# A gated retention and conv mixer: rotation by swapped copies, centred values, and another order of small steps

## The reference

```python
p = h @ w_in
rq, rk, rv, rg, gq, gf, gi, gg, ca, cb, gates = jnp.split(p, bounds, axis=-1)
q = _rope(heads(rq, 4), positions)            # t1*cos - t2*sin, t1*sin + t2*cos
k = _rope(heads(rk, 4), positions) * (128 ** -0.5)
o = _retention(q, k, heads(rv, 4))            # sum_{s<=t} gamma_h^(t-s) (q_t.k_s) v_s
mu = o.mean(-1, keepdims=True)
o = (o - mu) * lax.rsqrt(jnp.square(o - mu).mean(-1, keepdims=True) + LN_EPS)
u_a = o * ret_norm_g * jax.nn.silu(rg)

o = _hgrn2(silu(gq), logf, -expm1(logf), gi)  # S_t = diag(f_t) S_{t-1} + k_t v_t^T, o_t = S_t^T q_t
o = o * lax.rsqrt(jnp.square(o).mean(-1, keepdims=True) + LN_EPS)
u_b = o * hgrn_norm_g * jax.nn.silu(gg)

u = _causal_dwconv(ca * jax.nn.sigmoid(cb), conv_w, conv_b)   # 31 taps
u_c = jax.nn.silu(_layer_norm(u, conv_ln_g, conv_ln_b))
y = sum over three branches of sigmoid(gates[:, :, i]) * (u_i @ w_branch[i])
return y @ w_out
```

## Time and profile before

| | us |
|---|---|
| median of 3 runs | 3512.76 (3499.04 to 3517.75) |
| the profiled execution | 3506.1 |
| its span, first to last instruction | 3504.3 |

### The profile page before, as it was taken

One profiled execution on the slowest core, in us unless ns is written; L12 is line 12 of the kernel. 1 busy time (PEld: TensorE's weight loads), 2 busy tenths in 40 slices (PEclk: granted clock), 3 DMA queues, 4 the chain that ended last, 5 costly groups with the idle time before them and its releaser, 6 DMA issues. The chain is left out here.

```text
span 3504.3 us, 38804 instructions
## 1 busy us (share of the span) xinstructions
PE 3335.8 (95%) x15280; PEld 2662.9 (76%) x15280; DVE 2126.9 (61%) x2701; ACT 1306.1 (37%) x1684; POOL 616.4 (18%) x496
## 2 busy tenths in 40 slices
PE   8899999999999999989999998999898999989997
PEld 6577788886677788877777876888676777768886
DVE  8853566448654766477556746554676557465545
ACT  4664322234663322233332234243433322343323
POOL 2222222121212212201000132010201001320002
PEclk9999999999999999999999999999999999999999
DMA  4122555322123454232112222222221112222221
GB/s 133 37 68 85 186 192 192 108 96 65 39 78 132 181 192 168 91 112 72 61 55 66 91 99 89 96 96 93 75 85 60 61 55 90 96 73 96 97 97 71
DMA packets 72180, 344.43 MB, mean 98 GB/s; under 512 B 25152, under 2 KB 26048, under 8 KB 35648
## 3 DMA queue, kind: packets, MB, share of 16 engines
q1 hardware_dynamic: 70416, 339.12, 28.2%
q0 software_dynamic: 576, 2.33, 0.2%
q10 hardware_dynamic: 1008, 0.51, 0.1%
HBM read 340.51 MB, written 2.10 MB: 98 GB/s over the span
## 5 line engine op out<-in xcount | busy, mean ns | idle before, releaser
L893 PE MATMUL bank<-Hhi_b,whi_b 128*128 128x512 f32 x2976 | 1220.2, 410 | 62.3 <-ACT Hhi_b L2048 22.1
L894 PE MATMUL bank<-Hhi_b,wlo_b 128*128 128x512 f32 x2976 | 1170.5, 393 | 0.0
L900 PE MATMUL bank<-Hlo_b,whi_b 128*128 128x512 f32 x2976 | 1160.9, 394 | 0.8 <-DVE Hlo_b L2329 0.8
L871 DVE TENSOR_TENSOR wlo_b<-raw_b,whi_b 128x2048 fp32r<-128x2048 f32 (+2 forms) x290 | 626.6, 2161 | 487.7 <-ACT whi_b L865 487.5
L893 PEld LDWEIGHTS bank<-Hhi_b,whi_b 128*128 128x128 f32 x2976 | 566.3, 190 | 212.8 <-issue 43.7
L894 PEld LDWEIGHTS bank<-Hhi_b,wlo_b 128*128 128x128 f32 x2976 | 566.6, 190 | 125.4 <-issue 13.8
L900 PEld LDWEIGHTS bank<-Hlo_b,whi_b 128*128 128x128 f32 x2976 | 563.9, 190 | 124.9 <-DVE Hlo_b L2329 4.2
L865 ACT ACTIVATE whi_b<-raw_b 128x2048 fp32r<-128x2048 f32 (+2 forms) x290 | 511.6, 1764 | 368.4 <-PE bank L900 364.4
L893 PE MATMUL bank<-Uhi_b,whi_b 128*128 128x512 f32 x1024 | 405.7, 396 | 11.3 <-POOL Ulo_b L982 11.3
L894 PE MATMUL bank<-Uhi_b,wlo_b 128*128 128x512 f32 x1024 | 399.8, 390 | 0.0
L900 PE MATMUL bank<-Ulo_b,whi_b 128*128 128x512 f32 x1024 | 386.2, 390 | 0.0
(11 more groups left out here) (257 smaller groups left out, 3460.3 us busy)
## 6 DMA issues: line engine op xcount, KB each, us to landing
raw_b<-in_w SPq DMA_DIRECT2D x234, 1024.0 KB, 4.9
ada_b<-in_wada SPq DMA_DIRECT2D x48, 1024.0 KB, 7.0
raw_b<-in_w SPq DMA_DIRECT2D x40, 512.0 KB, 3.8
raw_b<-in_w SPq DMA_DIRECT2D x16, 768.0 KB, 4.3
rel_b<-in_rel SPq DMA_DIRECT2D x128, 24.0 KB, 2.4
X_keep<-in_x SPq DMA_DIRECT2D x4, 512.0 KB, 9.5
decay_b<-in_decay POOLq DMA_DIRECT2D x2, 1024.0 KB, 6.9
out<-X_keep SPq DMA_DIRECT2D x8, 256.0 KB, 2.0
```

The source lines that it names most:

```text
L871: self.nc.vector.tensor_tensor(self.wlo[n % RAW_SLOTS][:, 0:words], self.raw[n % RAW_SLOTS][:, 0:words], self.whi[n % HI_SLOTS][:, 0:words ...
L893: self.nc.tensor.matmul(out, whi[:, k, cols], xhi, start=(k == 0), stop=False)
L894: self.nc.tensor.matmul(out, wlo[:, k, cols], xhi, start=False, stop=False)
L900: mm = self.nc.tensor.matmul(out, whi[:, k, cols], xlo, start=False, stop=(k == nk - 1))
```

## The change

- The rotation matmul goes. On evacuation of an rq or rk chunk, ACT copies the upper half of the partitions, negated, to the lower half of a new buffer `qr`, and the lower half to the upper, and then the whole to `qf`. The "rrot" item is issued right there: POOL multiplies `qf` by cos in place, DVE multiplies `qr` by sin in place and adds the two.
- The "omean" group goes. The four transposes of a retention head's values become plain matmuls of the same tiles with the matrix (identity - 1/128), so that the head's output has mean zero over its channels. The square is taken by ACT from the bank ahead of the copy.
- The head's end has three parts: "oss" without the reciprocal, "orec" (the reciprocal) and "oend". When another head follows, "orec" joins its second group and "oend" its fourth; behind the last gated head they are groups of their own with an empty one between. `finish` no longer takes these two.
- Taps: one beside each group of a retention head, where it was two (one at "oss"); one beside the levels 1, 3, 5 and 7, where it was none; "orec" ahead of its group takes the free number.
- The gate and projection panels of branch 0 all come ahead of those of branch 1.

The diff, cut to its core:

```diff
-    return heads, mixed(0, 0) + mixed(1, 0) + mixed(0, 1) + mixed(1, 1), mixed(2, 0) + mixed(2, 1)
+    return heads, mixed(0, 0) + mixed(0, 1) + mixed(1, 0) + mixed(1, 1), mixed(2, 0) + mixed(2, 1)
 def taps_beside(group, free):
-    if not kinds or kinds == ["oend"]:
+    if not kinds or kinds[0] == "orec":
         return free
...
-    if group[0][2] == "r":
-        return 1 if "oss" in kinds else 2
-    return 0
+    if kinds[0] == "level":
+        return group[0][4] % 2
+    return 1 if group[0][2] == "r" else 0
...
         def finish(branch, h):
-            while any(item[2:4] == (branch, h) for group in chain for item in group):
+            while any(item[2:4] == (branch, h) and item[0] not in ("orec", "oend") for group in chain for item in group):
                 step()
         def follow(*groups):
-            if chain and chain[-1][0][0] == "oend":
-                groups = (groups[0] + chain.pop(),) + groups[1:]
+            if chain and chain[-1][0][0] == "orec":
+                orec, oend = chain.pop()
+                groups = groups[:1] + (groups[1] + (orec,), groups[2], groups[3] + (oend,)) + groups[4:]
             chain.extend(groups)
...
             s.add("evp", l, t, i)
+            if t in ("rq", "rk"):
+                run(("rrot", l, "r", i, t))
...
-                    first = [(item("rrot", "rq"),), (item("rrot", "rk"),), (item("vt2"),)]
-                    first += [(item("rscore", j),) for j in range(TT)] + [(item("rpv"),), (item("omean"),)]
+                    first = [(item("vt2"),)]
+                    first += [(item("rscore", j),) for j in range(TT)] + [(item("rpv"),)]
...
-                follow(*first, (item("oss"),), (item("oend"),))
+                follow(*first, (item("oss"),), (item("orec"), item("oend")))
+                if (b, i) == ("h", 3):
+                    orec, oend = chain.pop()
+                    chain.extend(((orec,), (), (oend,)))
... (POOL, "rrot")
-                ng.tensor_tensor(buf(("t1", l, b, h, t)), buf(("qf", l, t, h)), cos[:], ALU.mult)\
+                ng.tensor_tensor(q, q, cos[:], ALU.mult).then_inc(*mark("pool", ("q cos", l, t, h)))
... (ACT, "evp")
+                elif t in ("rq", "rk"):
+                    half = P // 2
+                    reuse(act, qr_)
+                    act_e.activation(buf(qr_)[0:half], z[half:P], ACT.Copy, scale=-1.0)\
+                        .then_inc(*mark("act", ("qr low", l, t, i)))
+                    act_e.activation(buf(qr_)[half:P], z[0:half], ACT.Copy).then_inc(*mark("act", qr_))
+                    reuse(act, qf_)
+                    act_e.activation(buf(qf_), z, ACT.Copy).then_inc(*mark("act", qf_, ("free", job)))
... (DVE, "rrot")
-                nv.tensor_tensor(t2[:], k.out_of(rot)[:], sin[:], ALU.mult)\
-                nv.tensor_tensor(buf(name), u, t2[:], ALU.add)\
+                dve.wait_ge(*after("qr", l, t, h))
+                nv.tensor_tensor(v, v, sin[:], ALU.mult).then_inc(*mark("dve", ("q sin", l, t, h)))
+                dve.wait_ge(*after("q cos", l, t, h))
+                dve.wait_ge(*after("q sin", l, t, h))
+                nv.tensor_tensor(buf(name), u, v, ALU.add)\
... (DVE: "omean" goes; "oss" keeps the scaling of ON)
-                k.root(None, dve, ("oss", l, b, h), rs, 1.0 / P, EPS2)
+            elif kind == "orec":
+                l, b, h = a
+                k.root(None, dve, ("oss", l, b, h), ("rs", l, b, h), 1.0 / P, EPS2)
... (PE: "rrot" and "omean" go)
-                nt.matmul(k.out_of(job)[:], rot128[:], buf(("qf", l, t, h)), start=True, stop=True)\
-                nt.matmul(k.out_of(job)[:], keep.ones[:], ON[:], start=True, stop=True).then_inc(*mark("pe", job))
                 for t in range(TT):
-                    mm = nt.transpose(k.out_of(job)[:, tile(t)], buf(v)[:, tile(t)], keep.ident[:])
+                    if b == "r":
+                        mm = nt.matmul(k.out_of(job)[:, tile(t)], buf(v)[:, tile(t)], center[:], start=True, stop=True)
+                    else:
+                        mm = nt.transpose(k.out_of(job)[:, tile(t)], buf(v)[:, tile(t)], keep.ident[:])
... (host)
+    center = (np.eye(P) - 1.0 / P).astype(np.float32)
```

More of the change, by code:

```diff
@@ L622, in evacuate @@
                 s.temp("qf", 4, ("qf", l, t, i))
+                s.temp("qr", 2, ("qr", l, t, i))
             if t in ("rv", "gi"):
@@ L1732, in block_two @@
     um = mem.again(ulo_at + 4 * SEQ * 4, ulo_at + 8 * SEQ * 4)
-    t1 = [um.put(f"t1{i}", [P, SEQ]) for i in range(2)]
-    t2 = um.put("t2", [P, SEQ])
+    qr = [um.put(f"qr{i}", [P, SEQ]) for i in range(2)]
+    um.at += SEQ * 4
     pos_i = um.put("pos_i", [P, SEQ], I32)
```

71 lines of the change are left out of this document (19 added, 52 removed).

## The result

The median fell from 3512.53 us (3499.04 to 3517.75, four runs) to **3449.44 us** (3448.62 to 3450.02, four runs); the ratio is 0.9831, with a 95% interval of 0.9808 to 0.9853. The forecast was 3443, inside 3420 to 3466. The profiled execution took 3449.65 us against 3506.1, so 56.5 us less; the medians differ by 63.1. The 6.6 us between them come from the kernel before, whose runs scatter by 18.7 us and whose profiled execution lies 6.4 us (0.18%) under its median, while the new kernel's lies on it.

A forecast was written before the change was run, and what follows sets the result against it. PE, busy 95%, was taken as the bound. Matmuls (18.2 us) plus waits and tails (27.1 in layer 0, 24.5 in layer 1) made 69.8 off 3506.1; 3436.3 times 1.0019 (profile to median) gave 3443 us, range 3420 to 3466.

The forecast's parts named there:

- ACT: Rotation evacuation: three copies instead of one, +1.1 us 16 times, costed at nothing on PE; 18 us without cover.
- The rotation's waits: First scores' waits for the rotated key: 5.8 us go in layer 0 and 7.0 in layer 1.
- The forced steps of "finish": PE's waits for the square, 1.91 us at a retention head and 1.3 behind the first gated head: 3.2 us a layer go.
- The reciprocal: Moved behind level 1 of the next gated head: waits fall from 8.9 to 4.1 us a layer, 4.8 gone.
- Rival A: The reciprocal only moves; waits return at levels 2 and 3, so the levels gain nothing: 3462 us, chance 0.17.
- First branch together: First panel reading the gated heads' split comes four panels later; its 3.50 us wait for POOL goes in both layers.
- The start of layer 0: Mixer's first panels: panel 3 starts 2.7 us later, yet 1.8 us of excess goes besides the matmuls; bounds -2.7 and +4.
- New waits: DVE late at heads 0 and 2: 1.5 us in layer 0, 3.5 in layer 1; range 0 to 10.
- rival D: DVE stands at each of 16 rotations for ACT and POOL, delaying queued work 4.0 us plus tail: 3531 us, chance 0.02.
- The tails: Slow products after PE's long waits, 16 and 15 us in the two layers: 9.5 us of each go.
- Rival C: Each of 16 sine multiplies on DVE waits 1.6 us more for POOL's cosine, PE with it: 3469 us, chance 0.06.
- B: Only the matmuls' 18.2 us count; every wait removed comes back elsewhere: 3495 us, chance 0.06.

The follow-up runs named there:

- the added matmuls: Changed kernel with each head's sum of squares computed twice, 8 more fp32 matmuls a layer: 3460.65 us, 0.9862 of the kernel before.
- The five undone parts: Changed kernel with one part put back each: gate order 3461.86 us, tap numbers 3469.70, two-part head's end 3468.05, rotation in the chain 3461.44, mean step 3457.89.

## Why the prediction was right or wrong, point by point

**The number.** 3449.44 against 3443 is nearer than the working deserves. In the profiled executions 56.5 us came of 69.8, a miss of 13.3, and in the mixers 52.8, a miss of 17.0. The first block's 3.7 us made up for some of it. The factor 1.0019 made up for 6.9: it added 6.7 us for a profiled execution under its median, and the new kernel's lies 0.2 above. So nearly two thirds of the miss in the mixers don't show in the median, by luck. In the sum itself, 24 x 0.90 is 21.6 and not 21.7, and the spread's lower end comes to 3436 by the bounds that are given, not 3432; neither matters.

**Matmuls.** Right. No rotation or mean matmul is left, the centring costs 0.90, and the added matmuls cost 0.855 each. By these prices about 18 of the 52.8 us are this part. No run puts the rotation's matmuls back alone.

**ACT.** Right. The half copies cost 596 ns each, and with three copies instead of one the cover held: no wait of PE in the new kernel is put down to a rounding. What was overlooked is that DVE can stand for these copies (0.58 us ahead of the sine multiply at 1581.37).

**The rotation's waits.** Right in mechanism: the row of RK is gone, and putting the operations back brought 8.1 us of such waits, though none for head 3. Undoing the place cost 6.5 and 3.1 us net.

**The forced steps of "finish".** The waits for the square ahead of a head's buffers are gone as said. They weren't tried by themselves; one for head 1's square comes back with the mean's group, for another reason.

**The reciprocal.** Right, a little optimistic. Forecast were 1.2, 1.2 and 1.7 us at level 3; idle were 1.35, 1.34 and 1.94, and with the excess beside them 1.6, 1.6 and 2.2. That is 1.3 us a layer more than the 4.1 of the sum. Rival A fell: the two-part end costs 13.3 and 6.9 us, 7.3 and 5.7 of them at the levels.

**First branch together.** The wait went in both layers. Undoing it cost 6.2 us a layer where 3.5 stood in the sum, since the tail goes with it. Some was given back: 1.07 us at the end of the last head, and slow products of 1.5 us behind the first panel of branch 2, whose wait was there before.

**The start of layer 0.** Forecast was panel 3 some 2.7 us later than 1565.7; it started at 1565.19. Since the second block began 3.76 us earlier, that is 44.7 us into the mixer against 41.5, 3.2 later. But 1.6 of these were lost before any rotation: the first twelve products took 4.42 us at a granted clock of 0.61, against 2.84 at 1.00 before. The wait ahead of panel 3 grew by 1.6, from 7.72 to 9.30. In the kernel with the added matmuls, whose first products ran fast, panel 3 starts 43.8 us into the mixer, 2.3 later. So the order on DVE did what was said, at 1.6 to 2.3 us instead of 2.7. The excess of this part is 11.3 us where the sum had 13.3: the tail was shorter, 2 us better.

**New waits: the step that failed.** The sum had 1.5 us in layer 0 and 3.5 in layer 1. Measured in layer 0 are 1.62 (output of head 0), 1.56 (panel of head 2) and 2.43 (output of head 2), 5.6 us. Layer 1 has 3.4 + 1.6 of idle time and a tail of 1.7, 6.7 us. Together 12.3 us, above the range of 0 to 10 that was given to them. The prediction said that PE's next need from DVE is usually a panel away, and used this against rival D. For the keys of heads 1 and 3 it is false: the last score of the head before is in the same piece, and its multiply is issued behind the rotation. Issuing the rotation behind the group took these waits away, fewer free taps took the one at head 2's panel. What I had put down to free taps, rotations and the reciprocal meeting in one panel was thus two causes at two places. It is 7.3 us of the 17 that were missed.

**The tails.** 19 us were to go with their waits. Slow products aren't booked as waits, so they are only known as excess less idle time: the earlier trace rows gives 16 and 15 us before, and now 8.9 and 9.8 (33.2 less 24.3 idle, 26.8 less 17.0). About 12 of the 19 went. Three places got tails of 1.5 to 1.7 us instead: the new wait for head 2's output in layer 1, and the old waits ahead of the third branch and of the first product in layer 0.

**Summed up for layer 0.** The forecast excess was 52 - 27.1 = 24.9 us, and 33.2 were measured. Of the 8.3 between them: output of head 0 1.6, head 2's two places 2.5 above the 1.5 allowed, levels 1.3, small waits of gated head 0 at level 1 and at its output 1.9, the last head's end 1.1, the slow products at branch 2 1.5; less 2.0 at the start. That is 7.9. The 1.6 us of the first twelve products aren't in it; with them it is 9.5, so the items are known to about 1 us in all.

**Rival C** was right in kind and a quarter of its price at most: three of the 16 sine multiplies were 1.09 us longer, and taking POOL away gave 6.4 us over both layers where C had 25.6. The 6.4 include what came of DVE's waits at the add, 2.6 and 3.9 us. **B** fell, since far more went than 18 us.

**The parts aren't additive.** The five undone parts cost 42.1 us in layer 0 together, and 27.8 is all that the change gave there, rotation matmuls included. In layer 1 they cost 26.4 together, and the change gave 25.0 there. So in layer 0 at least, a part undone alone costs more than its share of the whole. Tails that come and go are some of it; that a lateness on DVE adds to those around it would explain the rest, but is only argued: the parts weren't tried one by one on the kernel before.

## What to carry to other kernels

Where every engine walks one list, put an operation that waits for two other engines behind the group that the busiest engine wants in the same piece, and count what is queued behind it before calling its place free: moving an early rotation by one group was worth 7.7 us over both layers. Filler work (taps) needs a number per step that leaves its engine level with the panel's needs; it was among the dearest things here to get wrong, 9.4 us a layer on the mean for the taps beside the heads' groups and 6.5 for those beside empty steps. Don't give every wait a tail: one of 2.1 us cost 2.1 or 3.8 here, in one and the same kernel. That moves the measured price of a known amount of work too: 6.8 us of matmuls added to a layer cost 5.6 in one and 2.7 in the other. So a part is better priced from the starts around its own place than from the whole stretch.

## What the runs showed of the hardware that was not expected

- A matmul group behind a wait of 2.12 us took 4.09 us at a granted clock of 0.56 in one kernel and 2.39 us at 1.00 in another, with the same wait. Within one kernel both happened behind the same wait, by layer.
- Copies of 64 partitions from a bank to the other half of the partitions cost ACT 596 and 592 ns, as much as the whole tile's 601.
- An fp32 multiply of two SBUF tiles on DVE took 1.78 us where it started while POOL's multiply was under way (two of eight in layer 0) and 0.69 us otherwise.
